# One-hot rows of the expert gates: one instruction of VectorE per token with two per-partition scalars, in place of a compare on VectorE and a multiplication on GpSimd

## The reference, cut to what matters

```python
expert = jnp.take_along_axis(cand_id, pos, axis=-1)      # 8 x 16 numbers per token, each i * 128 + j
gate = jax.nn.softmax(top_s, axis=-1)
...
ug = u_tab[ec]
vg = v_tab[ec]
act = jax.nn.gelu(jnp.einsum('thkd,td->thk', ug, xc).astype(jnp.float32), approximate=False)
w = (gc * act).astype(vg.dtype)
return jnp.einsum('thk,thkd->td', w, vg)
```

## Time and profile before

| | |
|---|---|
| median of three executions | 1792.36 us (1786.25 to 1793.43) |
| the profiled execution | 1799.46 us, span 1797.6 us |
| PE busy | 1699.4 us, 95% of the span |
| DVE busy | 1262.7 us, 70% |
| ACT busy | 1020.1 us, 57% |
| POOL busy | 77.2 us, 4% |
| mean granted TensorE clock | 0.981 of full |
| time in the chain of waits | PE 89%, DVE 5%, ACT 2%, issue 2%, DMA 2% |

### The profile page before, as it was taken

How to read it: one execution, slowest core, us unless ns; L and a number is a source line. 1 busy time by engine, 2 the same in 40 slices (tenths; PEclk the granted TensorE clock), 3 DMA queues, 4 the chain that set the end, 5 groups by cost and what they waited for, 6 DMA issues and landing times.

```text
span 1797.6 us, 31061 instructions
## 1 busy us (share of the span) xinstructions
PE 1699.4 (95%) x9982; PEld 1429.1 (80%) x9982; DVE 1262.7 (70%) x2545; ACT 1020.1 (57%) x2016; POOL 77.2 (4%) x74
## 2 busy tenths in 40 slices
PE   7898999999999888899999999988999999899997
PEld 6764998888888655688888888966888879888886
DVE  5446559989996699866666676457676666767666
ACT  5444556666666688555555554337565555446553
POOL 0000000000000165200000000000000000000000
PEclk9989999999999899999999999999999999999999
DMA  6545445555555588555565654410365554545552
GB/s 236 195 153 175 152 154 188 180 188 185 185 187 186 198 279 284 193 192 195 191 219 190 196 190 150 161 36 1 112 199 190 190 199 147 158 142 191 192 188 94
DMA packets 86935, 316.34 MB, mean 176 GB/s; under 512 B 9664, under 2 KB 9808, under 8 KB 86352
## 3 DMA queue, kind: packets, MB, share of 16 engines
q1 hardware_dynamic: 85248, 309.30, 51.6%
q10 hardware_dynamic: 1328, 4.01, 0.6%
q0 software_dynamic: 288, 2.10, 0.3%
HBM read 314.32 MB, written 1.05 MB: 175 GB/s over the span
## 4 chain that ended last, share of the span: by engine, by line
PE 89%; DVE 5%; ACT 2%; issue 2%; DMA 2%; POOLq 0%; ACTq 0%; DVEq 0%
PE acc L495 21%; PE bank L505 20%; PE bank L495 11%; PE acc L496 10%; PE bank L506 10%; PE bank L496 5%; PE bank L884 4%; PE acc L606 3%; PE bank L627 1%; DMA route<-in_ada_w 1%; ACT arena L1141 1%; DVE small L2176 1%; PE bank L846 0%; DVE w_lo L1665 0%; ACT L1141 0%
## 5 line engine op out<-in xcount | busy, mean ns | idle before, releaser
L1665 DVE TENSOR_TENSOR w_lo<-raw,w_hi 128x512 fp32r<-128x512 f32 x982 | 667.4, 690 | 413.2 <-ACT w_hi L1141 410.9
L1141 ACT ACTIVATE w_hi<-raw 128x512 fp32r<-128x512 f32 x982 | 614.8, 632 | 549.3 <-PE acc L495 252.8
L505 PE MATMUL bank<-x_both,w_hi 128*128 128x512 f32 x1532 | 544.2, 400 | 2.8 <-DVE x_both L2288 2.8
L506 PE MATMUL bank<-x_both,w_lo 128*128 128x256 f32 x1532 | 430.9, 281 | 0.0
L505 PEld LDWEIGHTS bank<-x_both,w_hi 128*128 128x128 f32 x1532 | 288.6, 188 | 75.5 <-issue 3.2
L506 PEld LDWEIGHTS bank<-x_both,w_lo 128*128 128x128 f32 x1532 | 290.2, 189 | 0.5
L495 PE MATMUL bank<-x_both,w_hi 128*128 128x256 f32 x1384 | 256.1, 287 | 14.3 <-DVE w_lo L1665 10.2
L495 PEld LDWEIGHTS bank<-x_both,w_hi 128*128 128x128 f32 x1384 | 218.7, 194 | 19.4 <-issue 10.5
L495 PE MATMUL acc<-w_hi,x_both 128*128 128x512 f32 x560 | 219.6, 392 | 3.9 <-DVE w_lo L1665 2.5
L495 PE MATMUL acc<-w_lo,x_both 128*128 128x512 f32 x560 | 218.9, 391 | 0.0
L496 PE MATMUL acc<-w_hi,x_both 128*128 128x512 f32 x560 | 218.9, 391 | 0.0
(11 more groups left out here) (260 smaller groups left out, 1824.4 us busy)
## 6 DMA issues: line engine op xcount, KB each, us to landing
raw<-in_peer_u SPq DMA_DIRECT2D x128, 512.0 KB, 3.5
raw<-in_peer_v SPq DMA_DIRECT2D x128, 512.0 KB, 4.2
raw<-in_mlp_w SPq DMA_DIRECT2D x128, 512.0 KB, 3.5
ada_x<-in_ada_w SPq DMA_DIRECT2D x64, 512.0 KB, 4.2
route<-in_ada_w SPq DMA_DIRECT2D x32, 512.0 KB, 6.0
raw<-in_w_in SPq DMA_DIRECT2D x25, 512.0 KB, 4.5
raw<-in_conv_w_in SPq DMA_DIRECT2D x24, 512.0 KB, 4.3
raw<-in_attn_w_in SPq DMA_DIRECT2D x18, 512.0 KB, 3.5
```

The source lines that it names most:

```text
L505: first = mm(ps[:, :], w[0], x_joined[:, :, c * T:(c + 1) * T], start=(c == 0), stop=False, **kw)
L506: return first, mm(ps[:, 0:T], w[1], x_hi[:, c * T:(c + 1) * T], start=False, stop=(c == KC - 1), **kw)
L1141: return nc.scalar.activation(dst, src, f, **kw)
L1665: v.tensor_tensor(w_lo[:, unit(n, half)], raw[:, a:a + HALF], w_hi[:, unit(n, half)].bitcast(F32), ALU.subtract).then_inc(s["lo_done"], 1)
```

## The change

Three things are edited.

1. The comparison with `iT` and the multiplication by `gT` become one instruction: `tensor_scalar` with two scalars that are read per partition, `(iota == i) * gate`. Such a scalar is one number per partition, so an instruction can serve one token only: four instructions of 128 columns take the place of one of 512. The fourth signals `gated_i`.
2. GpSimd's loop of 64 multiplications is gone, and with it the semaphore `eq_i`.
3. The rows of j that VectorE makes (g = 3 and 7) are also made by four `tensor_scalar` of 128 columns, with one scalar and no second operation.

```diff
-            with pool.Fori(0, 8) as i:
-                for g in range(8):
-                    pool.wait_ge(s["eq_i"], i * 8 + (g + 1))
...
-                    nc.gpsimd.tensor_tensor(e, e, gT[:, bass.ds(i * 32 + 4 * g, 4)].unsqueeze(2).to_broadcast([P, 4, P]),
-                                            ALU.mult).then_inc(s["gated_i"], 1)
...
-            def one_hot(dst, index, token):
-
-                shape = [P, 4, P]
-                return v.tensor_tensor(dst.rearrange("p (t k) -> p t k", t=4), C("iota").unsqueeze(1).to_broadcast(shape),
-                                       index[:, bass.ds(token, 4)].unsqueeze(2).to_broadcast(shape), ALU.is_equal)
...
+            def gated_one_hot(g, token):
+
+                for t in range(4):
+                    a = g % 4 * 512 + t * P
+                    last = v.tensor_scalar(ione[:, a:a + P], C("iota"), iT[:, bass.ds(token + t, 1)], gT[:, bass.ds(token + t, 1)],
+                                           ALU.is_equal, ALU.mult)
+                last.then_inc(s["gated_i"], 1)
+
+            def one_hot_j(token):
+
+                for t in range(4):
+                    last = v.tensor_scalar(jone[:, 512 + t * P:512 + (t + 1) * P], C("iota"), jT[:, bass.ds(token + t, 1)], None,
+                                           ALU.is_equal)
+                last.then_inc(s["one_jd"], 1)
...
             for g in range(3):
-                one_hot_i(g, 4 * g)
+                gated_one_hot(g, 4 * g)
             with dve.Fori(0, 8) as i:
                 for g in range(8):
-                    one_hot_i(g + 3, i * 32 + 4 * (g + 3))
+                    gated_one_hot(g + 3, i * 32 + 4 * (g + 3))
                     if g % 4 == 2:
-                        one_hot(jone[:, 512:1024], jT, i * 32 + 4 * (g + 1)).then_inc(s["one_jd"], 1)
+                        one_hot_j(i * 32 + 4 * (g + 1))
```

More of the change, by code:

```diff
@@ L113 @@
     exps_ready qk_gla_ready at_zeroed moba_sq_ready head_rstd
-    moba_tables sm1_max sm1_exp sm1_p moba_o_full sq2_ready route_done gate_exp gate_ready eq_i one_j one_jd j_sq
+    moba_tables sm1_max sm1_exp sm1_p moba_o_full sq2_ready route_done gate_exp gate_ready one_j one_jd j_sq
     gated_i silu_c mod_ready v_full gated_hi gated_lo lam_in attn_v_full attn_v_ready b_sq b_rstd b_rope
@@ L1620, in _ @@
             nc.gpsimd.memset(at_sb, 0.0).then_inc(s["at_zeroed"], 1)
-            with pool.Fori(0, 8) as i:
-                for g in range(8):
-                    pool.wait_ge(s["eq_i"], i * 8 + (g + 1))
-                    e = ione[:, (g % 4) * 512:(g % 4 + 1) * 512].rearrange("p (t k) -> p t k", t=4)
-                    nc.gpsimd.tensor_tensor(e, e, gT[:, bass.ds(i * 32 + 4 * g, 4)].unsqueeze(2).to_broadcast([P, 4, P]),
-                                            ALU.mult).then_inc(s["gated_i"], 1)
             pool.wait_ge(s["v_full"], 7)
@@ L2017, in _ @@
             v.tensor_tensor(lamw[:, 1:2], V("lam", 2), V("lam", 3), ALU.mult).then_inc(s["lam_in"], 1)
-            def one_hot(dst, index, token):
-                shape = [P, 4, P]
-                return v.tensor_tensor(dst.rearrange("p (t k) -> p t k", t=4), C("iota").unsqueeze(1).to_broadcast(shape),
-                                       index[:, bass.ds(token, 4)].unsqueeze(2).to_broadcast(shape), ALU.is_equal)
-            def one_hot_i(g, token):
-                one_hot(ione[:, g % 4 * 512:(g % 4 + 1) * 512], iT, token).then_inc(s["eq_i"], 1)
+            def gated_one_hot(g, token):
[9 more added lines that the diff above has]
+                last.then_inc(s["one_jd"], 1)
             for g in range(3):
-                one_hot_i(g, 4 * g)
+                gated_one_hot(g, 4 * g)
             with dve.Fori(0, 8) as i:
                 for g in range(8):
-                    one_hot_i(g + 3, i * 32 + 4 * (g + 3))
+                    gated_one_hot(g + 3, i * 32 + 4 * (g + 3))
                     if g % 4 == 2:
-                        one_hot(jone[:, 512:1024], jT, i * 32 + 4 * (g + 1)).then_inc(s["one_jd"], 1)
+                        one_hot_j(i * 32 + 4 * (g + 1))
                     wait_full(dve, "g", g, i * 2)
```

## The result

The changed kernel takes 1796.28 us (median of 20 executions, 1791.45 to 1798.88), the kernel before 1791.34 (20 executions on the same chips, 1786.25 to 1798.67). The ratio is 1.0025, with a 95% interval of 1.0014 to 1.0036: slower by about 4.5 us, and within the 0.5% that was named as no change. The forecast was 4 us slower.

A forecast was written before the change was run, and what follows sets the result against it. VectorE, the slow part of a ring with TensorE, was taken to bound the stage of the gates. Its period goes from 7.35 to 7.61 us, over 15.75 periods plus 4 us: 1796.4 us, range 1786 to 1814.

The forecast's parts named there:

- The ring of VectorE and TensorE: Stage of the gates: TensorE waits for group 3's j, VectorE for group 0's product; VectorE still waits 0.26 us per period.
- nothing but the stage pays: After the stage of the gates TensorE is full, so what the stage gives or takes passes to the end unchanged.
- rival 3: VectorE's comparison runs at one column per cycle: 0.32 and 0.26 us per instruction, period 8.68, plus 21 us, 1813; chance 0.14.
- Rivals 1 and 2: VectorE's new instructions: all scalars free, minus 14 us, 1778, chance 0.09; only the second free, minus 3, 1789, chance 0.08.
- a rule of the Trainium skill: VectorE's fixed 58 cycles plus columns by mode, no scalar term: 127 ns per new instruction, 20 of them 2.5 us.
- The register feed: VectorE's queue: two register addresses per instruction need an estimated 0.13 to 0.19 us, covered by 0.255 us of engine work.
- rival 4: VectorE's queue can't feed its instructions: 0.32 us for two scalars, period 8.39, plus 16 us, 1809; chance 0.11.
- The trade: In VectorE's stage, saving from quiet GpSimd about equals new fixed parts; one wait kept, period 7.61 for 7.35, plus 4 us.
- the first step: Profile slices: VectorE at nine tenths in slices 14 to 17, well below elsewhere, so the stage has its own bound.

The follow-up runs named there:

- e4: Changed kernel with the four rows of j moved ahead of the rows of i in the same turn; 1794.32 us, ratio 0.9998 to the kernel before.
- e3: Changed kernel with the comparison's one scalar only, gates left out, a minimum in place of the product with the bank; 1788.34 us, ratio 0.9973.
- e1: Kernel before without GpSimd's 64 multiplications, gates not applied, VectorE taking a minimum in place of the product; 1782.26 us, ratio 0.9948.
- e5: Changed kernel with the third edit undone: VectorE's rows of j are one comparison of 128x512 again; 1792.05 us, ratio 1.0004.
- e2: Changed kernel with GpSimd doing 64 bystander multiplications into a buffer nobody reads; 1837.74 us, ratio 1.0251.
- e7: Kernel before with the row of j moved ahead of the row of i in the same turn; 1797.48 us, ratio 1.0028.
- e8: Changed kernel with the gate moved to j in group 1 (ScalarE) and group 3 (VectorE) of four, their i rows wide; 1796.74 us, ratio 1.0017.
- e10: The same kernel as e8, run once more; 1792.40 us, ratio 1.0016 to the kernel before.

## Why the prediction was right

**The bound.** The ring of VectorE and TensorE was read from two views laid side by side, and e4 confirms it: the rows of j earlier, the wait gone, 0.3 us less in each period. That nothing but the stage pays is confirmed too: from the first row to the first multiplication it is 4.8 us in both profiles, and behind the stage 1055.0 and 1055.2.

**The prices.** Two scalars at 128 columns were not to be seen before; 0.255 us came from the row with 256 columns less 0.067. Measured: 0.256. One scalar 0.20: measured 0.196. Both are as cheap as multiplications of the same form, so a comparison costs nothing extra and rival 3 (0.32 and 0.26) falls. Rivals 1 and 2 fall by the same rows, and e3 shows the 0.06 us of the second scalar. The prediction also weighed a rule of the Trainium skill ("VectorE: DVE Perf Modes", "The TRN2 errata — SBUF-src ops pay a fixed extra latency per instruction"), from which it estimated 127 ns for each new instruction. The trace does not agree: 0.256 us. What differs is mostly the scalars that are read per partition: without them the prediction's estimate from the earlier trace rows is 0.14 us.

**The register feed.** 93 ns of DVE's queue for two addresses, less than the estimate of 0.13 to 0.19 us. No idle time of DVE stands between neighbours of L2016 in the profile after (they start 0.236 to 0.259 us apart); rival 4 falls.

**The trade.** The text said that the saving from a quiet GpSimd was about as large as the new fixed parts. The runs give both: rows without GpSimd's disturbance 47.0 us (e1), so 23.2 saved; the narrow rows 76.8, so 29.8 paid. Net 6.6, less 1.3 of wait and 0.7 of multiplications: 4.6 us in the stage, and about 4.5 by the ratio of the medians.

**What was off.** Nothing that the sum rests on. But the busy share of VectorE did not single out the stage, as the first step had it: the slices of the earlier trace rows are at 8 and 9 tenths from the seventh to the twelfth too. There PE is busy all the time (269.70 of 269.70 us from 269.6 to 539.3), and what marks the stage of the gates is that PE is not. The prediction also calls 0.13 us the fixed part and 0.06 more the price of each scalar; by its own rows the 0.13 already hold the first scalar, and the fixed part without any is 0.07. Its prices of 0.20 and 0.255 are not touched by this.

The third edit went into the sum rightly, but nobody asked whether it helps; it is 3 of the 4.5 us (e5). And GpSimd's disturbance is no fixed price of each multiplication, as the expectation of e2 had it; e7 shows that it hangs on what VectorE does at that moment: 23.2 us in one order, 33.9 in the other.

## What to carry to other kernels

Before cutting a wide instruction with broadcasts into narrow ones with scalars per partition, price the narrow form from start to start: here 0.07 us fixed, 0.06 for each of two scalars and 0.067 for 128 columns made 0.256 us, or 1.02 for four, against 0.60 for the wide comparison alone. What GpSimd costs VectorE is seen in the spread of one instruction's durations (0.68 to 1.53 us), and it depends on the order of the instructions: a wait that looks wasted may be where the other engine's work was harmless. In a ring of two engines, make what the other one waits for first, and what is needed only three groups later after it (e4: the stage is 4.4 us shorter). But look at what else leans on the old order: with GpSimd at work the same move made the stage 4.4 us longer (e7).

## What the runs showed of the hardware beyond the prediction

- GpSimd's multiplication of two SBUF inputs stretches VectorE's `tensor_scalar` of one tensor as much as its `tensor_tensor` of two: 0.35 us per GpSimd instruction in e2, 0.37 in the kernel before. VectorE's product with a PSUM bank is not stretched (medians of 0.699 in e2 and 0.702 in the changed kernel).
- Of a row of VectorE and a multiplication of GpSimd the one that starts second is stretched: in the kernel before, 16 rows that ran when GpSimd's instruction began kept 0.68 us, and that instruction took 1.32 us (median) in place of 1.04; 61 rows that began behind one had a median of 0.915.
- With the second engine beside it and longer holes in TensorE's work, the mean granted clock fell from 1.00 to 0.83 for the whole stage (e2), at the lower level once in each period, and the loss doubled.
- Four ScalarE Relus of 128 columns with scale and bias per partition take 1.64 us (e8, e10), four squares with a bias alone 1.28.
- For VectorE a scalar that is read per partition costs 0.06 us in an instruction, a second operation with a constant about 0.01 at most.
